# Seven-product pairs for the gate and up blocks of the second gated feed-forward

## The reference

```python
def swiglu(x, w_gate, w_up, w_down):
    return (jax.nn.silu(x @ w_gate) * (x @ w_up)) @ w_down
...
        h = h + jnp.concatenate([attn_o, gla_o], axis=-1) @ w_out[i]
        h = h + 0.5 * swiglu(rmsnorm(h, ffn2_norm[i]), ffn2_w_gate[i], ffn2_w_up[i], ffn2_w_down[i])
        gate = jax.nn.sigmoid(rmsnorm(h, ple_gate_norm[i]) @ ple_w_gate[i])
        emb = rmsnorm(p[i] @ ple_w_proj[i], ple_norm[i])
        h = h + gate * emb
...
def sq_relu_mlp(h, w1, w2):
    u = jax.nn.relu(h @ w1)
    return (u * u) @ w2
```

## Time and profile before

| | us |
|---|---|
| median of 3 runs | 2253.64 (2253.39 to 2257.74) |
| the profiled execution | 2255.11 |
| its span, first to last instruction | 2253.3 |
| PE busy | 2224.9 (99%) |
| DVE busy | 1337.6 (59%) |
| ACT busy | 892.6 (40%) |
| POOL busy | 321.0 (14%) |

### The profile page before, as it was taken

One profiled execution on the slowest core, in us unless ns is written; L12 is line 12 of the kernel. 1 busy time (PEld: TensorE's weight loads), 2 busy tenths in 40 slices (PEclk: granted clock), 3 DMA queues, 4 the chain that ended last, 5 costly groups with the idle time before them and its releaser, 6 DMA issues.

```text
span 2253.3 us, 30491 instructions
## 1 busy us (share of the span) xinstructions
PE 2224.9 (99%) x12660; PEld 1855.0 (82%) x12667; DVE 1337.6 (59%) x1562; ACT 892.6 (40%) x1190; POOL 321.0 (14%) x191
## 2 busy tenths in 40 slices
PE   9999999999999999999999999999999999999999
PEld 7888888878888888888886789899876858898998
DVE  6434446597644345475557675576567874855754
ACT  4222234345422332353238543344434574533532
POOL 2000001030100100021002123123100301231230
PEclk9999999999999999999999999999999999999999
DMA  5233322320233323232320133333333201334332
GB/s 190 94 94 94 111 75 86 101 72 20 84 99 107 93 94 93 76 111 94 113 75 20 55 107 111 122 112 104 99 115 80 72 20 45 115 112 122 106 110 94
DMA packets 201186, 208.12 MB, mean 92 GB/s; under 512 B 7042, under 2 KB 195218, under 8 KB 201076
## 3 DMA queue, kind: packets, MB, share of 16 engines
q1 hardware_dynamic: 201076, 206.56, 29.6%
HBM read 199.27 MB, written 2.10 MB: 89 GB/s over the span
## 4 chain that ended last, share of the span: by engine, by line
PE 91%; DVE 6%; ACT 2%; issue 1%; DMA 0%; SPq 0%; ACTq 0%; DVEq 0%
PE psum L867 78%; PE psum L957 4%; PE psum L955 4%; PE psum L956 4%; DVE sm L2880 1%; DVE w_lo L404 1%; DVE rstd L2287 0%; PE psum L1409 0%; PE psum L1401 0%; DVE free_x L2269 0%; ACT w_hi L391 0%; ACT free_h L1685 0%; DVE free_h L2272 0%; DVE free_x L3002 0%; DVE sm L3000 0%
## 5 line engine op out<-in xcount | busy, mean ns | idle before, releaser
L867 PE MATMUL psum<-xg_lo,w_hi 128*128 128x512 f32 (+1 forms) x1576 | 608.5, 389 | 0.4 <-ACT free_x L1685 0.4
L867 PE MATMUL psum<-xg_hi,w_hi 128*128 128x512 f32 (+1 forms) x1528 | 596.2, 390 | 3.9 <-DVE xg_lo L2269 1.7
L867 PE MATMUL psum<-xg_hi,w_lo 128*128 128x512 f32 (+1 forms) x1528 | 592.9, 388 | 0.0
L391 ACT ACTIVATE w_hi<-w_raw 128x2048 fp32r<-128x2048 f32 (+1 forms) x148 | 281.6, 1903 | 382.9 <-PE psum L867 363.3
L404 DVE TENSOR_TENSOR w_lo<-w_raw,w_hi 128x2048 fp32r<-128x2048 f32 (+1 forms) x146 | 340.9, 2335 | 151.2 <-ACT w_hi L391 148.0
L867 PEld LDWEIGHTS psum<-xg_lo,w_hi 128*128 128x128 f32 x1576 | 295.6, 188 | 62.2 <-ACT free_x L1685 1.4
L867 PEld LDWEIGHTS psum<-xg_hi,w_hi 128*128 128x128 f32 x1528 | 287.0, 188 | 68.0 <-issue 4.9
L867 PEld LDWEIGHTS psum<-xg_hi,w_lo 128*128 128x128 f32 x1528 | 286.9, 188 | 59.5
L867 PE MATMUL psum<-h_hi,w_hi 128*128 128x512 f32 x696 | 278.1, 400 | 3.1 <-DVE w_lo L404 2.8
L867 PE MATMUL psum<-h_hi,w_lo 128*128 128x512 f32 x696 | 271.8, 391 | 0.0
L867 PE MATMUL psum<-h_lo,w_hi 128*128 128x512 f32 x696 | 271.8, 390 | 0.0
(11 more groups left out here) (347 smaller groups left out, 3468.8 us busy)
## 6 DMA issues: line engine op xcount, KB each, us to landing
w_raw<-in_mlp_w SPq DMA_DIRECT2D x36, 1024.0 KB, 5.2
w_raw<-in_ffn_w_gate SPq DMA_DIRECT2D x21, 1024.0 KB, 5.3
w_raw<-in_ffn_w_up SPq DMA_DIRECT2D x21, 1024.0 KB, 5.3
w_raw<-in_mlp_w SPq DMA_DIRECT2D x42, 512.0 KB, 4.9
w_raw<-in_ffn_w_down SPq DMA_DIRECT2D x16, 1024.0 KB, 5.1
w_raw<-in_diff_w_in SPq DMA_DIRECT2D x12, 1024.0 KB, 5.1
w_raw<-in_w_in SPq DMA_DIRECT2D x9, 1024.0 KB, 5.2
w_raw<-in_dsa_w_in SPq DMA_DIRECT2D x9, 1024.0 KB, 5.2
```

Of the source, the lines that this page charges most:

```text
L391: e.activation(w_hi[:, wside(c), 0:n], w_raw[:, c % 2, 0:n], ACT.Copy).then_inc(sem("hi_done"), 1)
L867: return pe.matmul(out, lhsT, rhs, start=start, stop=stop)
```

## The change

`ffn2` joins `FAST`. Its first pair stays plain (`PLAIN`), the other 3 + 4 + 3 = 10 pairs become seven-product pairs, with the up block as first and the gate block as second block of a pair. `fast_gated` on ACT and on DVE carries their evacuation: the first halves are joined in `buf_a`, scaled in place (`gate_scaled`), silu is done in place, `buf_b` collects the up part, is multiplied by `buf_a`, and becomes `h_hi`, `h_lo`. POOL makes the sums with `fast_sums("ffn2", ...)`; in group 1, `add_squares` of the embedding stands between the first sum and the others. `X_WITH` gets a row for `wout1`, the projection ahead of `ffn2`, equal to that of `wout2`. In group 1, the load of `w_third` waits for `emb_ssq` 7. The embedding input goes to `buf_c` (its parts to `buf_a` and `buf_b`), loaded among the `down` loads of group 0 by `load_p`; the other embedding buffers, constants at the start and the rms values are moved in memory with no work added; `emb_rms` uses PSUM bank 6 instead of 5. `arena` grows by 3584 floats per partition.

```diff
-FAST = ("mlp0", "mlp1")
+FAST = ('ffn2', 'mlp0', 'mlp1')
+PLAIN = {"ffn1": 2, "ffn2": 1, "mlp0": 1, "mlp1": 1}
+STAGE = {"ffn1": 0, "ffn2": 2, "mlp0": 5, "mlp1": 7}
...
-        arena = sb("arena", [P, 10752])
-        p_hi = nc.alloc_sbuf_tensor_at("p_hi", [P, 2, S], F32R, offset=arena_at + 9728 * 4)
-        p_lo = nc.alloc_sbuf_tensor_at("p_lo", [P, 2, S], F32R, offset=arena_at)
-        p_raw = arena[:, 0:1024].rearrange("p (k t) -> p k t", t=S)
+        arena = sb("arena", [P, 14336])
+        p_hi = nc.alloc_sbuf_tensor_at("p_hi", [P, 2, S], F32R, offset=buf_a_at)
+        p_lo = nc.alloc_sbuf_tensor_at("p_lo", [P, 2, S], F32R, offset=buf_b_at)
+        p_raw, pos_int, pos_row = buf_c, ssq[0:1, :].bitcast(I32), ssq[0:1, :]
...
         w_run = [arena[:, 8192 + 1024 * i:9216 + 1024 * i] for i in range(2)]
+        consts = arena[:, 10240:14336]
...
-        X_WITH = {"wout2": ((), (0, 1), (2,), ()), "wout3": ((0,), (1,), (2,), ())}
...
+        X_WITH = {"wout1": ((), (0, 1), (2,), ()), "wout2": ((), (0, 1), (2,), ()), "wout3": ((0,), (1,), (2,), ())}
...
+            def load_p(buffer_free):
+
+                sp.wait_ge(sem("ms"), 3)
+                sp.dma_start(pos_int, io["positions_2"]).then_inc(sem("p_in"), 16)
+                sp.wait_ge(*buffer_free)
+                sp.dma_start(p_raw[:], io["p"].rearrange("(k p) t -> p k t", p=P)).then_inc(sem("p_in"), 16)
+
+            def fast_loads(c0, p, blocks, third_free=None):
...
                     if q == 0:
-                        sp.wait_ge(sem("ssq_done"), 7 * (p + 1))
+                        sp.wait_ge(*(third_free or (sem("ssq_done"), 7 * (p + 1))))
                     else:
                         sp.wait_ge(*strip_mark("lo", c0, 7 * (q - 1) + 4))
                     half(w_third, w2, 0, sem("w21_third_in"))
...
+                    if wg is not None and name in FAST:
+                        vg, vu = (rows(w, 0, KT)[:, :, P * f0:P * (f0 + tiles)] for w in (wg, wu))
+                        ahead = PLAIN[name] if g == 0 else 0
+                        for j in range(skip, ahead):
+                            load(sp, c + 2 * j, 0, vg[:, :, j * BC:(j + 1) * BC])
+                            load(sp, c + 2 * j + 1, 0, vu[:, :, j * BC:(j + 1) * BC])
+                        fast_loads(group_first[name, g], p, lambda q: (vu[:, :, (q + ahead) * BC:(q + ahead + 1) * BC],
+                                                                       vg[:, :, (q + ahead) * BC:(q + ahead + 1) * BC]),
+                                   (sem("emb_ssq"), 7) if (name, g) == ("ffn2", 1) else None)
...
+                            if (name, g, i) == ("ffn2", 0, 1):
+                                load_p((sem("u_read"), fast_groups[c0][-1] + 1))
...
-                        fast_up(c + 2 if g == 0 else c, p)
+                        for j in range(1, PLAIN[name] if g == 0 else 0):
+                            blk(c + 2 * j, a=xg(p))
+                            blk(c + 2 * j + 1, a=xg(p))
+                        fast_up(group_first[name, g], p)
...
                     pe.wait_ge(sem("emb_ssq"), 7)
-                    mm(bank[5], mean[:], emb_sum).then_inc(sem("emb_stat"), 1)
+                    mm(bank[6], mean[:], emb_sum).then_inc(sem("emb_stat"), 1)
```

ACT:

```diff
+            def fast_gated(c0, p, h0, s0, ahead, of_plain):
...
+                    t = 2 * (q + ahead)
+                    act.wait_ge(sem("hmul"), h0 + q + 1)
+                    a(hidden(p)[0][:, t:t + 2, :], buf_b[:], ACT.Copy).then_inc(sem("h_hi_done"), 1)
+
+                for q in range(len(made)):
+                    split(7 * q + 3)
+                    silu(q - 1)
+                    copy(q, 0)
+                    split(7 * q + 4)
+                    hidden_hi(q - 1)
+                    copy(q, 1)
+                    split(7 * q + 5)
+                    copy(q, 2)
+                    for n in range(6, 10):
+                        split(7 * q + n)
+                q = len(made) - 1
+                hi(act, after)
+                silu(q)
+                hidden_hi(q)
+                hi(act, after + 1)
+
             def ffn(name, groups, p, gated, p_next, between=None, before_down=None):
-                if name in FAST:
+                if name in FAST and p:
...
+                        if ahead:
...
+                            act.wait_ge(sem("evac"), c0 - 1)
+                            a(buf_c[:], buf_a[:], ACT.Silu).then_inc(sem("silu"), 1)
...
+                            for n in range(2, 4):
+                                strip_hi(act, c0, n)
+                        fast_gated(c0, p, h0 + ahead, s0 + ahead, ahead, plain_hi)
```

DVE:

```diff
+            def fast_gated(c0, p, h0, s0, ahead, of_plain):
...
+                def last_quarter(q):
+                    if q >= 0:
+                        dve.wait_ge(*strip_mark("pe", c0, 7 * q + 6))
+                        tt(buf_b[:, :, TS:S], by_halves(pair_banks(c0, q)[0]), scale[:, :, TS:S], ALU.mult).then_inc(sem("evac"), 1)
+
+                def gate_up(q):
+                    if q >= 0:
+                        dve.wait_ge(sem("evac"), c0 + 2 * q + 2)
+                        dve.wait_ge(sem("silu"), s0 + q + 1)
+                        tt(buf_b[:], buf_b[:], buf_a[:], ALU.mult).then_inc(sem("hmul"), 1)
+
+                def hidden_lo(q):
+                    if q < 0:
+                        if ahead:
+                            of_plain()
+                        return
+                    t = 2 * (q + ahead)
+                    dve.wait_ge(sem("h_hi_done"), h0 + q + 1)
+                    tt(hidden(p)[1][:, t:t + 2, :], buf_b[:], hidden(p)[0][:, t:t + 2, :].bitcast(F32),
+                       ALU.subtract).then_inc(sem("h_done"), 1)
+
+                for q, pair in enumerate(made):
+                    run, side_sum, first_sum = pair_banks(c0, q)
+                    last_quarter(q - 1)
+                    split(7 * q + 3)
+                    gate_up(q - 1)
+                    split(7 * q + 4)
+                    hidden_lo(q - 1)
+                    split(7 * q + 5)
+                    split(7 * q + 6)
+                    dve.wait_ge(*strip_mark("pe", c0, 7 * q + 3))
+                    dve.wait_ge(sem("h_done"), h0 + q)
+                    tt(buf_b[:, :, 0:TS], by_halves(first_sum), scale[:, :, 0:TS], ALU.mult)
+                    split(7 * q + 7)
+                    dve.wait_ge(*strip_mark("pe", c0, 7 * q + 4))
+                    tt(buf_a[:, :, TS:S], by_halves(run), by_halves(buf_c[:, q % 2, :]), ALU.add).then_inc(sem("u_read"), 1)
+                    split(7 * q + 8)
+                    if q == len(made) - 1:
+                        if len(made) % 2:
+                            lo_half(dve, after, 0, odd_turn[c0])
+                        else:
+                            lo(dve, after)
+                    dve.wait_ge(*strip_mark("pe", c0, 7 * q + 5))
+                    tt(buf_a[:, :, 0:TS], by_halves(side_sum), by_halves(buf_d[:, q % 2, :]), ALU.add).then_inc(sem("evac"), 1)
+                    if q == len(made) - 1 and len(made) % 2:
+                        lo_half(dve, after, 1, odd_turn[c0])
+                    dve.wait_ge(sem("u_read"), pair + 1)
+                    dve.wait_ge(sem("evac"), c0 + 2 * q + 1)
+                    stt(buf_a[:], buf_a[:], -1.0, scale, ALU.mult, ALU.mult).then_inc(sem("gate_scaled"), 1)
+                    split(7 * q + 9)
+                q = len(made) - 1
+                last_quarter(q)
+                gate_up(q)
+                hidden_lo(q)
...
+                            evac_scaled(c0 - 2, buf_a)
...
+                            evac_scaled(c0 - 1, buf_b)
+                            dve.wait_ge(sem("evac"), c0)
+                            dve.wait_ge(sem("silu"), s0 + ahead)
+                            tt(buf_d[:], buf_b[:], buf_c[:], ALU.mult).then_inc(sem("hmul"), 1)
+                            for n in range(2, 4):
+                                strip_lo(dve, c0, n)
+                        fast_gated(c0, p, h0 + ahead, s0 + ahead, ahead, plain_lo)
```

POOL, and the scratch size:

```diff
+            def first_sum(c0, q):
+
+                pair, c = fast_groups[c0][q], c0 + 2 * q
+                pool.wait_ge(sem("w21_in"), 16 * (pair + 1))
+                pool.wait_ge(sem(f"landed{c % 2}"), 16 * (c // 2 + 1))
+                add_rows(w_run[run_half[pair]], raw(c, 0), sem("w_first"))
+
+            def other_sums(c0):
+
+                made = fast_groups[c0]
+                for q, pair in enumerate(made):
+                    c = c0 + 2 * q
+                    pool.wait_ge(sem("w22_in"), 16 * (pair + 1))
+                    pool.wait_ge(*strip_mark("lo", c0, 7 * q + 1))
+                    add_rows(w_run[run_half[pair]], raw22(c0, q), sem("w_next"))
+                    pool.wait_ge(sem("w21_third_in"), 16 * (pair + 1))
+                    add_rows(w_third, raw22(c0, q), sem("w_third"))
+                    if q + 1 < len(made):
+                        first_sum(c0, q + 1)
```

(15 more changed lines are left out.)

175 lines of the change are left out of this document (113 added, 62 removed).

## The result

The changed kernel takes 2265.37 us (median of 7 runs, 2261.5 to 2266.4), beside 2255.21 for the kernel before on the same chip. The ratio is 1.0042, 95% interval 1.003 to 1.0054 (all ratios here are taken like this): slower by 0.4%, where I had forecast 0.2% faster, with 2254.5 as the upper end. The profiled execution took 2264.07 us, its span is 2262.3.

A forecast was written before the change was run, and what follows sets the result against it. PE's instruction stream was taken as the bound. Terms -18.3 + 4.4 + 8.4 + 0.5 gave -5.0 us: the profiled 2255.11 would become 2250.1, the median of 2253.64 become 2248.7, range 2243 to 2254.5.

The forecast's parts named there:

- The steady pairs: In ffn2's seven-product pairs, DVE needs some 15 of 19.94 us; no holes: 0, upper end 0.3 us a pair.
- Rival D: Gated pairs of ffn2 held by scaling, silu, product, high and low part; at 1.5 us a pair +10, 2263.6; chance 0.08.
- saving on PE: Ten ffn2 pairs go from 96 matmuls of 512 columns to 168 of 256: 1.83 us each, 18.3 saved.
- start of `ffn2`: Activation sums in wout1 delay the next split: a 2.94 us hole, 1.50 of low clock, cost 4.4 us.
- start of group 1: Product 2 waits for ACT's copy, behind the embedding's squares: hole 6.95 us, 1.5 of low clock, cost 8.4 us.
- Group 2's first pair: Start of group 2: ACT's sine tables end before its first copy is due, cost 0, with little to spare.
- The tail of group 2: Last pair's evacuation against a down block of 8.16 us: the chain ends near 8.6, cost 0.5 us.
- rival C: More start-up holes at group 0 or 2 or behind group 1's first pair: -3 to +3, about 2252.5; chance 0.12.

The follow-up runs named there:

- the sums thin: The changed kernel with POOL's weight sums for ffn2's seven-product pairs made over only 64 of 1024 columns, the rest left out of the result: 2246.29 us, ratio 0.9962.
- two spread-out orders: The changed kernel with wout1's preparation steps of activation sums one each behind two evacuations (2264.09 us), or behind three, together with other edits (2248.82 us).
- the squares on DVE: The changed kernel with the embedding's seven square additions on DVE instead of POOL, and the fourth strip's raw half loaded earlier: 2260.3 us, ratio 1.0025.

## Why the prediction was wrong

**The failing step is "The steady pairs", its term of 0 for holes.** It put DVE at 15 us of 19.94, and 14.8 is what it is with the sums thin. What it left out is POOL. "POOL's four sums of 2.4 us leave half its time" reads an engine's idle time as if the two engines had nothing in common; in a middle pair the sums cost DVE 6.8 us more, 21.6 in all. The term was 0 with 3 as the upper end for ten pairs; it measured 14.2 us for the four middle pairs (3.84, 2.52, 3.98, 3.84 above 19.94; 8.6 of it are the holes, and 4.8 the slower products behind three of them), 0.9 for the last pairs and 1.8 for the first of group 2, together 16.9. The thin sums took 17.0.

**Rival D gave the sign and the size, for half of the reason.** It said 2263.6 at 1.5 us a pair, a size taken as an example; that 1.7 came, and 2265.4, is in part luck, since 14.2 of the 16.9 us lie in four of the ten pairs. Against it I wrote that the window of `mlp0` already holds the effect of POOL. It does not hold this pattern: `mlp0` has groups of one and two such pairs, so each is a first or a last one. In its two pairs POOL makes five additions, never four in a row. And the effect stood in the trace of before, in a view that I did not read. DVE in time, kernel before, second pair of that window:

```profile
1396.45 2.38 DVE L2272 SCALAR_TENSOR_TENSOR buf_a<-buf_a,rstd 128x1024 f32<-128x1024 f32 x1
1398.88 3.31 DVE L346 TENSOR_TENSOR w_lo<-arena,w_hi 128x1024 fp32r<-128x1024 f32 x1
1402.11 0.68 DVE L2272 SCALAR_TENSOR_TENSOR buf_b<-psum,rstd 128x512 f32<-128x512 f32 x1
1402.71 3.12 DVE L346 TENSOR_TENSOR w_lo<-w_raw,w_hi 128x1024 fp32r<-128x1024 f32 x1
```

Three additions, three operations of 1.22 us that last 2.4 to 3.3, 1.7 us more each. So the 33.01 us of `mlp0` held 5.1 us of stretching, and the 15 of the gated pair, added up from single operations, held none. From these rows the sum would have been 14.8 + 4 x 1.7 = 21.6 us for a middle pair of 19.94, and D the likeliest case. With 0.08 it was priced by an argument where a row was to be had.

**Right: saving on PE.** Hole-free pairs last 19.94 us in `ffn2` as in `mlp0`; 168 matmuls of 256 columns and no less.

**Right: start of `ffn2`.** A hole of 2.79 us, and 12.64 for the first block in place of 10.88: 4.5 against 4.4. That two spread-out orders gave almost nothing back shows that it is no matter of order alone; that DVE has more steps than fit behind these blocks is my reading, and no run takes steps away.

**Nearly right: start of group 1.** The hole was 4.78 us (I had 6.95), released by ACT's copy as forecast; the half landed about 5 us after its issue at 748.5, not 6.5. The pair lost 7.3 us against 8.4: the shorter hole was partly made up by the low clock behind it, 2.3 us (5.15 for the third product in place of 2.83) where I had 1.5. With the squares on DVE the loss is 2.2.

**Wrong and small.** Group 2's first pair: I took 0, and named ACT's sine tables as the late thing. It was DVE's angles, which POOL's additions stretched too, and strip 2's low part behind them: 1.8 us. The tail of group 2 cost 0.3 against 0.5. Two slips of arithmetic, neither of which matters: with hand-overs of 0.1 the chain of that tail adds up to 8.8 and not 8.6, and the middle of rival C's -3 to +3 is 2253.6 and not 2252.5.

With the measured terms the sum is -18.3 + 4.5 + 7.3 + 16.9 + 0.3 = +10.7, beside +10.5 in the trace at the end of `ffn2`.

What stays open: whether `ffn2` has an arrangement in which the middle pairs reach 19.95 with the full sums. The best middle pairs with full sums are 20.5 us, and there DVE has no idle time left; so an order helps only if it lessens the stretching.
